# Context attention of a two-block transformer kernel: modulation weights multiplied unsplit, in fp32, on four column strips

## The reference, cut to what matters

```python
mod   = (silu(c)          @ w_mod[l] + b_mod[l])   # c: [1, 1024], w_mod[l]: [1024, 6*1024]
mod_c = (silu(c_ctx)[None] @ w_mod[l] + b_mod[l])
sh1, sc1, gt1, sh2, sc2, gt2 = split(mod, 6)       # and the same of mod_c
hc = rms_norm(ctx_s, g_norm1[l]) * (1 + csc1) + csh1
zc = hc @ w_in[l]
...                                                # attention over 256 context rows, 8 heads
gates = sigmoid(zc[..., OFF_G:])
m = g_conv * (y_conv @ w_conv_out) + g_four * (y_four @ w_four_out) + g_attn * (y_attn @ w_attn_out)
ctx_s = ctx_s + cgt1 * (m @ w_o)
```

## Time and profile before

| | us |
|---|---|
| median of 3 runs | 3194.05 |
| lowest and highest run | 3193.73, 3198.64 |
| span of the profiled execution | 3194.7 |
| its busy time: TensorE (PE) | 3145.5 |
| VectorE (DVE) | 2053.3 |
| ScalarE (ACT) | 1222.3 |

### The profile page before, as it was taken

How to read it: one execution, slowest core, us unless ns; L and a number is a source line. 1 busy time by engine, 2 the same in 40 slices (tenths; PEclk the granted TensorE clock), 3 DMA queues, 4 the chain that set the end, 5 groups by cost and what they waited for, 6 DMA issues and landing times.

```text
span 3194.7 us, 42423 instructions
## 1 busy us (share of the span) xinstructions
PE 3145.5 (98%) x16032; PEld 2637.5 (83%) x16032; DVE 2053.3 (64%) x2867; ACT 1222.3 (38%) x1780; POOL 0.2 (0%) x4
## 2 busy tenths in 40 slices
PE   8999999999999999999999999999999999999998
PEld 6889998787888888888788888868888878888886
DVE  6878886665687777656476555666544676664546
ACT  4664445454232223545332222444222266542221
POOL 0000000000000000000000000000000000000000
PEclk9999999999999999999999999999999999999999
DMA  7665552212344553211223233332222346323222
GB/s 276 209 205 163 181 171 94 66 49 78 112 139 133 176 185 119 93 60 53 80 79 106 94 97 98 99 119 93 99 96 96 112 80 76 70 81 105 93 98 73
DMA packets 103067, 359.72 MB, mean 113 GB/s; under 512 B 12152, under 2 KB 15360, under 8 KB 102912
## 3 DMA queue, kind: packets, MB, share of 16 engines
q1 hardware_dynamic: 101216, 354.41, 33.8%
q10 hardware_dynamic: 1696, 3.16, 2.1%
HBM read 349.14 MB, written 2.10 MB: 110 GB/s over the span
## 4 chain that ended last, share of the span: by engine, by line
PE 88%; DVE 6%; ACT 2%; issue 2%; DMA 0%; DVEq 0%; SPq 0%; ACTq 0%
PE ring L1728 25%; PE ring L1729 25%; PE ring L1730 25%; PE bank L1728 2%; PE bank L1730 2%; PE bank L1729 2%; DVE w_lo L2638 1%; PE ring L2069 1%; PE ring L2070 1%; PE bank L2094 1%; PE bank L2095 1%; PE bank L2275 1%; PE ring L2040 1%; ACT w_hi L941 1%; DVE x L3412 1%
## 5 line engine op out<-in xcount | busy, mean ns | idle before, releaser
L1728 PE MATMUL ring<-h_hi,w_hi 128*128 128x512 f32 (+1 forms) x2723 | 1004.2, 369 | 6.1 <-DVE h_lo L3407 2.1
L1729 PE MATMUL ring<-h_lo,w_hi 128*128 128x512 f32 (+1 forms) x2723 | 996.8, 366 | 0.0
L1730 PE MATMUL ring<-h_hi,w_lo 128*128 128x512 f32 (+1 forms) x2723 | 996.7, 366 | 0.0
L2638 DVE TENSOR_TENSOR w_lo<-raw,w_hi 128x1024 fp32r<-128x1024 f32 x590 | 720.6, 1224 | 274.5 <-ACT w_hi L941 261.3
L941 ACT ACTIVATE w_hi<-raw 128x1024 fp32r<-128x1024 f32 x590 | 622.0, 1056 | 682.7 <-PE ring L1730 665.6
L1728 PEld LDWEIGHTS ring<-h_hi,w_hi 128*128 128x128 f32 x2723 | 516.2, 190 | 94.3 <-issue 4.9
L1730 PEld LDWEIGHTS ring<-h_hi,w_lo 128*128 128x128 f32 x2723 | 515.8, 189 | 84.2
L1729 PEld LDWEIGHTS ring<-h_lo,w_hi 128*128 128x128 f32 x2723 | 516.6, 190 | 80.9
L1728 PE MATMUL ring<-y_hi,w_hi 128*128 128x512 f32 (+1 forms) x1456 | 537.6, 369 | 4.8 <-ACT z L1522 1.5
L1729 PE MATMUL ring<-y_lo,w_hi 128*128 128x512 f32 (+1 forms) x1456 | 534.5, 367 | 0.0
L1730 PE MATMUL ring<-y_hi,w_lo 128*128 128x512 f32 (+1 forms) x1456 | 534.4, 367 | 0.0
(11 more groups left out here) (386 smaller groups left out, 3052.2 us busy)
## 6 DMA issues: line engine op xcount, KB each, us to landing
raw<-ws SPq DMA_DIRECT2D x601, 512.0 KB, 3.4
z<-ws SPq DMA_DIRECT2D x52, 512.0 KB, 4.5
x<-ws SPq DMA_DIRECT2D x4, 512.0 KB, 10.1
x<-x_t SPq DMA_DIRECT2D x1, 2048.0 KB, 11.5
out_t<-x SPq DMA_DIRECT2D x8, 256.0 KB, 2.0
z<-xc ACTq DMA_DIRECT2D x6, 256.0 KB, 11.4
xc<-ctx_t SPq DMA_DIRECT2D x1, 1024.0 KB, 13.2
z<-ropes ACTq DMA_DIRECT2D x2, 512.0 KB, 4.2
```

Source lines behind the costliest of these rows:

```text
L1728: nc.tensor.matmul(o, a_hi, b_hi, start=start, stop=False)
L1729: nc.tensor.matmul(o, a_hi, b_lo, start=False, stop=False)
L1730: return nc.tensor.matmul(o, a_lo, b_hi, start=False, stop=stop)
L2638: nc.vector.tensor_tensor(w_lo[:, u, :], raw[:, u, :], f(w_hi[:, u, :]), ALU.subtract).then_inc(w_ready, 1)
```

## The change

Mod tiles of the context attention are no longer split. Each is multiplied by 4 fp32 matmuls instead of 8 fp32r ones: piece j of the tile (128 x 256) goes to the output partitions 32j to 32j + 31, with the 32 columns `c_wide[:, k, :]` (silu(c), silu(c_ctx) and 30 zeros) as weights. ACT and DVE only count their semaphores on for such a tile. ACT copies 128 instead of 4 partitions of sums, and the two tiny matmuls use the 128 x 2 matrix `quad_pair`, which adds the four strips. All matmuls of a mod tile are issued at its last eighth. The planner counts a mod tile as 5 x 256. SP may overwrite the slot of a mod tile only when TensorE is done with it: the load of tile t waits for `tile_done` of tile t - 4 where that is a mod tile. For this, the loop of loads is written out from tile 32 to tile 87. `c_parts`, `pair` and one wait on `lo_ready` go.

```diff
-        c_parts = sb("c_parts", [P, KB, 4], F32R)
-        pair = sb("pair", [4, 2])
...
-                cost = {"gate": 8 * 3 * self.T, "branch": 8 * 3 * self.T, "mod": 8 * 256}
+                cost = {"gate": 8 * 3 * self.T, "branch": 8 * 3 * self.T, "mod": 5 * 256}
...
-                return z[0:4, 15, half % 2 * 256:(half % 2 + 1) * 256]
+                return z[:, 15, half % 2 * 256:(half % 2 + 1) * 256]
...
-        raw_tiles = range(ab_first + AB_GAP, ab_first + AB_TILES)
+        ctx_attn = next(at0 for kind, layer, stream, at0 in steps if (kind, layer, stream) == ("attn", 0, "ctx"))
+        ctx_fill = fill_tiles(0, "ctx")
+        mod_tiles = tuple(ctx_attn + n for n, (kind, _) in enumerate(ctx_fill) if kind == "mod")
+        raw_tiles = frozenset(mod_tiles) | frozenset(range(ab_first + AB_GAP, ab_first + AB_TILES))
...
-            loads(FIRST + R, mid)
+            attn0 = ctx_attn // R * R
+            attn1 = -(-(ctx_attn + len(ctx_fill) + R) // R) * R
+            loads(FIRST + R, attn0)
+            for t in range(attn0, attn1):
+                if t - R in mod_tiles:
+                    sp.wait_ge(tile_done, t + 1)
+                load(t, ws[t], t - R + 1)
+            loads(attn1, mid)
...
-                            nc.scalar.activation(fl.rows(n // 2), fl.bank(fl.job[t])[0:4, 0:256],
+                            nc.scalar.activation(fl.rows(n // 2), fl.bank(fl.job[t])[:, 0:256],
                                                  ACT.Copy).then_inc(s_gate_read, 1)
...
                 columns(0)
-                pe.wait_ge(lo_ready, C.next(lo_ready))
...
-                        if k == 0:
+                        if k == 0 and kind == "mod":
+                            pe.wait_ge(loaded[c % R], 16 * ((c - FIRST) // R + 1))
+                        elif k == 0:
                             pe.wait_ge(w_ready, c + 1)
...
                         else:
-                            if (n % 2, k) == (0, 0):
+                            if k < 7:
+                                continue
+                            if n % 2 == 0:
                                 bank_free(job)
-                            weights = (w_hi, w_lo)[k % 2][:, c % R, k // 2 * 256:(k // 2 + 1) * 256]
-                            m = nc.tensor.matmul(fl.bank(job)[0:4, 0:256], c_parts[:, n % 2 * 4 + k // 2, :], weights,
-                                                 start=(n % 2, k) == (0, 0), stop=(n % 2, k) == (1, 7))
+                            for j in range(4):
+                                m = nc.tensor.matmul(fl.bank(job)[32 * j:32 * j + 32, 0:256], c_wide[:, n % 2 * 4 + j, :],
+                                                     raw[:, c % R, j * 256:(j + 1) * 256], start=n % 2 == 0, stop=n % 2 == 1)
...
-                                             pair[:, :], start=True, stop=True)
+                                             quad_pair[:, :], start=True, stop=True)
...
-            c_in = c_act[:, :].rearrange("p (s k) -> p k s", s=2)
-            both(c_in, c_parts[:, :, 0:2], c_parts[:, :, 2:4])
...
-            step(nc.vector.tensor_tensor(pair[:, :], ident[0:4, 0:2], ident[0:4, 2:4], ALU.add), consts)
```

More of the change, by code:

```diff
@@ L3714, in _ @@
             dve.wait_ge(s_mat, 16)
-            step(nc.vector.tensor_reduce(quad_pair[:, :], ident.rearrange("p (j c) -> p c j", j=4)[:, 0:2, :], AX_X, ALU.add))
-            step(nc.vector.tensor_tensor(pair[:, :], ident[0:4, 0:2], ident[0:4, 2:4], ALU.add), consts)
+            step(nc.vector.tensor_reduce(quad_pair[:, :], ident.rearrange("p (j c) -> p c j", j=4)[:, 0:2, :], AX_X, ALU.add),
+                 consts)
             step(nc.vector.tensor_copy(ones_r[:, :], ones))
```

## The result

The changed kernel takes **3231.34 us** (median of 4 runs, 3228.77 to 3232.02) against 3195.05 for the kernel before beside it: a ratio of **1.0109** [1.0096, 1.0123]. It is slower, as forecast, but by 36 us and not by 15, and the time lies above the range (3192 to 3223).

What follows compares the result with a forecast made beforehand. The prediction took TensorE to bound the kernel, busy 3145.5 of 3194.7 us. New waits of 33 less 10 for matmuls and 7 for splits gave +16, so 3210 us, with a range of 3192 to 3223.

Steps and rivals of the forecast that it cites:

- the twelve places: Gate or branch tiles whose slot held a pair's second tile: late load delays split, squash and next pair; 33 us.
- the load in front in the queue: The mod tile's load, freed 0.43 us earlier, goes first: 1.58 us more, landing 4.45 after issue instead of 3.3.
- only get more rows: Small edits: the columns matmuls, 0.64 us a group before, were said only to get more rows; no gain was counted.
- +33 new waits: SP's new slot wait: TensorE waits summed over twelve places to 33 us; 21 if loads land after 3.3 us.
- Nothing of it is in my sum: TensorE's clock may fall in the new waits; left out of the sum, up to 12 x 1.0 to the upper end.
- I take 7 us: Splits taken off ACT (34 us) and DVE (39 us): TensorE recovers 7 us of waits, between 4 and 9.
- Landed at 4.7: The late tile lands 4.7 us after PE's last slot of the pair; 4.3 where max_row parts the pair.
- The waits place by place: Waits at single gates: 2.9 at 3, 9, 32; 3.2 or 3.0 at 16, 45, 29, 35; 2.6, 2.8, 1.2 elsewhere.
- The load comes sooner: Rival, chance 0.20: loads land at 3.3 us or are met later; +4 and less, about 3197.
- the slot is not what ACT waits for: Rival, chance 0.13: the squash is not behind the landing, only gains are left; -17, 3178, halfway 3187.
- Serial strips: Rival, chance 0.03: the strips don't overlap at 256 columns, a pair takes 1.9 us longer; another 40 us, 3250.
- The clock falls at nearly every wait: Rival, chance 0.08: TensorE's clock falls at nearly all new waits; +26 to +28, 3221.

Runs made afterwards that it cites:

- late_load_only: The kernel before, with only SP's new wait: the load of tile t waits for TensorE where t - 4 is a mod tile; 3259.12 us, ratio 1.0206.
- squash_first: The changed kernel, but ACT squashes the gate just after a pair before splitting the next tile, and DVE subtracts later too; 3214.65 us, ratio 1.006.
- gate_load_first: The changed kernel, but SP asks for the late tile to be split before the mod tile ahead of it; 3216.76 us, ratio 1.0069.
- own_early: The changed kernel with 14 mod tiles in two buffers of their own and gate and branch loads moved ahead of mod loads; 3186.24 us, ratio 0.997.
- warm_fitted: The changed kernel with useless matmuls ahead of pairs and head values, as many as fit each wait of TensorE; 3225.72 us, ratio 1.0091.

## Why the prediction was right and wrong

**Right.** The direction and the mechanism: the slot that is free only after the multiplication (late_load_only), the twelve places, ACT meeting the split ahead of the squash (squash_first), and the load in front in the queue (gate_load_first). That the strips overlap at 256 columns was right too. PE at full clock in the kernel after, into and out of a pair:

```profile
94.04 0.28 PE L2081 MATMUL ring<-kv,y_lo 96*128 96x256 f32 x1
94.26 1.07 PE L2051 MATMUL ring<-raw,scr 128*32 128x256 f32 x16
95.26 0.39 PE L1736 MATMUL ring<-h_hi,w_hi 128*128 128x256 f32 x1
95.48 0.28 PE L1737 MATMUL ring<-h_lo,w_hi 128*128 128x256 f32 x1
```

From 94.04 to 95.48 are 1.44 us, less two ordinary slots of 0.12: a pair costs 1.20, predicted 1.13 (the distance of 0.22 behind the first product is part of the way out). The round trip is 0.35 over the 0.85 of the columns, not 0.28. The Trainium skill (TensorEngine Tiling (Array Packing), Key Properties) says that a change of mode drains TensorE, and the trace agrees, with 0.35 us for the round trip. (The prediction's 14.5 for a drain that costs nothing counts the round trip once a pair; with the three pairs that pay it twice it is 15.4 by its own figures.)

**Near in the sum, for other reasons: the matmuls.** own_early is busy 13.0 us less than the kernel before (115.4 to 102.4), where I had 10.0. The pairs don't give that: a whole one gains 1.81 - 1.20 = 0.61; one that a max_row parts costs 1.42 by the same reading (entry and exit twice) and gains 0.39; 13 x 0.61 + 3 x 0.39 = 9.1. Most of the rest is in the columns matmuls, of which the prediction said "only get more rows". PE in order of time, first the kernel before, then own_early twice: followed by the same product as there (L1728 before, L1755 here), and followed by a pair:

```profile
197.48 0.28 PE L1730 MATMUL ring<-h_hi,w_lo 128*128 128x256 f32 x1
197.69 0.60 PE L2052 MATMUL ring<-pair,z 4*128 4x2 f32 x4
198.22 0.39 PE L1728 MATMUL bank<-y_hi,kv 128*128 128x256 f32 x1
```
```profile
136.18 0.28 PE L1757 MATMUL ring<-h_hi,w_lo 128*128 128x256 f32 x1
136.31 0.51 PE L2086 MATMUL ring<-quad_pair,z 128*128 128x2 f32 x4
136.67 0.36 PE L1755 MATMUL bank<-y_hi,kv 128*128 128x256 f32 x1
...
97.02 0.50 PE L2086 MATMUL ring<-quad_pair,z 128*128 128x2 f32 x4
97.75 0.64 PE L2073 MATMUL ring<-raw,scr 128*32 128x256 f32 x8 [0.22 <-ACT scr L1544]
```

0.74 us from product to product before, 0.49 now: 0.25 less. I read that as a change of tile shape (4 rows before, 128 now) that the change took out; no run has the 4 rows alone. But in own_early only five of the 16 groups of columns have such a product behind them. Behind the other eleven comes a pair, and the pair has to wait for the squash: PE is busy for 0.51 us instead of 0.69, and then idle for 0.22 or more instead of 0.03 for most. From start to start nothing is gained there. In busy time the 16 groups fell from 10.8 to 7.5; with the pairs that is 12.4 of the 13.0 seen.

**The sum, term by term**, for the stage. Predicted: +33 new waits, -7 recovered, -10 matmuls, 0 clock: +16. Measured: 28.0 at the twelve places, 3.8 at b51, other waits 8.7 instead of 9.0, so -0.3; matmuls -13.0; busy time above that of own_early, 120.8 - 102.4, +18.4. That is **+36.9**, and the stage grew by 37.0; it has to come out so, since the terms are the parts of PE's idle and busy time. From the largest error down:

- *"Nothing of it is in my sum", of the clock. This is the step that failed most.* The text named the risk, priced a fall at 1.0 us, and gave 10 to the upper end (12 by its own words). The rows show a fall of over 6 us at half speed behind one wait (140 to 147), and 18.4 us more of busy time. Not all of it is loss: a gate that runs slowly while the load is under way only shortens the wait behind it. If landings 0.4 later than predicted add 12 x 0.4 = 5 to the 33, some 38 us of waits were due at full clock, and 28.0 were seen; so by this estimate about 10 of the 18.4 were hidden and 8 paid. The third that warm_fitted gives would be 6 to 7. Both are estimates: that the slow clock costs part of its 18.4 is supported, how much stays open.
- *"I take 7 us" for the splits taken off ACT and DVE, "between 4 and 9".* Measured 0.3. This and the next term, not the clock, put the time above the range, which had left 10 for the clock. Even in own_early, with all loads early, PE idles 11.8 us against 9.0, and the stage is 10.2 shorter, where matmuls and splits together were to give 17. Its branch tiles still wait 3.5 us for DVE and ACT (5.3 before), and eight waits of 0.22 for a squash are new. I had taken the engines' summed work for the cause. That a PE with 13 us less to do only arrives sooner at what it waited for fits this, but is argued. The relief is not worthless everywhere: in late_load_only, where ACT and DVE still split everything, the late loads cost far more.
- *"Twelve places".* There were thirteen. The tiles loaded behind the last pair of the stage belong to the next one, and I stopped counting at the stage's end; ACT meets their landing before it copies the last sums, and b51 waits 3.8 for that copy.
- *"Landed at 4.7".* Mean 5.1, and up to 6.2 at gate 45. The base of 3.3 held (gate_load_first), the load in front cost 1.5 and not 1.15. The mean hides two kinds: from issue to landing it was 4.2 to 4.8 at seven places, near the 4.45 predicted, and 5.6 to 6.0 at four. Why these four took longer stays open. Issuing is slower as well. SP's instructions for these tiles in the kernel after, 89 to 245 us (ns, min/median/max), where it was 332/333/333 before:

```profile
L869 SPq DMA_DIRECT2D raw<-ws x51: 327/372/1312, 95.0 to 239.8; - x51
```

- *The waits place by place* (3.2 at gate 45, 1.2 at 22, 2.8 at 19, 42, 48) came out as 5.2, 2.5, and 1.0, 0.7 and 1.3. The sum was near, 28.0 against 33, partly because the errors are of both signs.

**The rivals.** "The load comes sooner" and "the slot is not what ACT waits for" fell with the 69.1 us of ACT's waits. Serial strips fell with the pair of 1.20. "The clock falls at nearly every wait", +26 to +28, was the nearest in kind, and still 8 to 10 us short. The upper bound took the clock's 10 but left the recovery at 4 or more and the waits at 33 or less; with the recovery at 0 and the landing at 5.1 it would have been +38, above the result.

## What to carry to other kernels

To multiply a tile unsplit saves work on the engines that split, but keeps its ring slot until TensorE is through, and the next tile in that slot may be one that still has to be split. Look for who stands behind that landing in an engine's written order, and what stands behind that one; give the unsplit tiles buffers of their own and put the loads that somebody splits first in the queue. Here the same matmuls went from 1.1% slower to 0.3% faster by that alone. And when an edit puts waits of some us into a stage where TensorE was nearly always busy, the clock belongs in the sum, not beside it. Work taken off engines that are not the bottleneck goes into the sum only as waits that the trace names and that nothing else holds up.

## What the runs showed that I had not expected

- The clock did not follow the length of the last wait. After waits of 1.62 and 2.56 us the pair took 1.83 and 1.94, which is half speed; after 2.50 it took 1.07, full speed. Before the 1.62 there is another wait of 2.26 at 111.00, and before that one of 2.81. What decides it stays open.
- 12 matmuls before each late pair did not lift the stage's clock by more than 0.01 (0.86 to 0.87); 26 lifted it to 0.93 and fitted ones to 0.95.
- Column sums with 4 rows cost 0.25 us more, for two tiny matmuls (four records), than the same with 128 rows, where an ordinary product follows.
- Issuing a 512 KB load took SP up to 1.31 us, where before each took 0.33.
